# A hybrid decoder layer on one core: gates and scores in two row tiles of TensorE, another order of SyncE's loads, the last product by halves

## The chip, the cores and the metric

The kernel runs on one core of a Trainium2 chip. The metric is the device time of one execution in microseconds (us); lower is better. The engines are TensorE (PE, with PEld for its weight loads), VectorE (DVE), ScalarE (ACT), GpSimd (POOL) and SyncE (SP), which issues most DMAs. Each runs its own instruction stream in order; semaphores tie the streams together.

## The reference, cut to what matters

One layer on x of 2048 positions x 1024 channels, float32:

```python
h = rmsnorm(x, ln_gain);  z = h @ w_in                       # 1024 -> 4608 columns
q, k, v, g_attn, x_lru, g_lru = split(z)                     # 16 q heads, 4 kv heads, head_dim 64
q, k = partial_rope(q), partial_rope(k)
y_attn = swa_sink_attention(q, k, v, sinks) * silu(g_attn)   # window 128, blocks of 128
u = causal_depthwise_conv(x_lru, conv_w, conv_b)             # width 4
r = sigmoid(u @ w_r + b_r);  i = sigmoid(u @ w_i + b_i)      # 16 blocks of 64 x 64
a = exp(-8 * r * softplus(-lam))
h_t = a * h_(t-1) + sqrt(1 - a*a) * (i * u)                  # along the positions
y_lru = h * silu(g_lru)
out = rmsnorm(x + concat([rmsnorm(y_attn), rmsnorm(y_lru)]) @ w_out)
```

## The kernel before

**Precision.** Every product is made of float32 operands split in two parts, hi and lo, and takes three matmuls: hi x hi, hi x lo, lo x hi. The hi part is an ACT copy into the rounded type fp32r, the lo part a DVE (in places POOL) subtraction.

**Phase A** (`phase_a`) runs over 16 passes n: four quarters q of the sequence (512 positions) times four groups g (one kv head, four q heads, two 128-channel units u of the recurrent branch). A pass projects nine groups of 128 columns of w_in, each 24 matmuls of 128x512 (`project`, L1408): XL0, GL0, XL1 (inputs and gate of the recurrent branch), GA0, GA1 (attention gates), GL1, and KVG, Q0, Q1, which are already those of the next pass. In quarter 0 the weights come from w_in, are split on the chip (`split_w`) and both parts are stored to DRAM; from then on they are loaded back split. `split` and `split_next` tell the bodies which of the two it is. Results land in a ring of four PSUM banks, handed out by the list `R_XL0, R_GL0, ...`; `bank_free` waits until the user of the bank four places back has been drained.

TensorE's order in a pass is written out: XL0, GL0, XL1, score(0), gates(0), GA0, gates(1), score(1), GA1, turn_p(0), score(2), turn_x, GL1, weigh_v(0), turn_p(1), score(3), KVG, weigh_v(1), turn_p(2), Q0, weigh_v(2), turn_p(3), Q1, weigh_v(3), turn_v. turn_x transposes the next quarter's x; turn_p the probabilities of a block; weigh_v multiplies them by v.

- `score(b)` (L1437): per head two matmuls 128x128 by 128x256. `q_st` stacks the hi part of a head (64 rows) over its lo part, so that one matmul against k (k_hi stands twice, rows 0 to 63 and 64 to 127) yields two of the three products.
- `gates(u)` (L1469): two gates (r into bank R_R0/R_R1, i into R_I0/R_I1), three matmuls each. The weights of a gate are two blocks of 64x64 on the diagonal of a 128x128 tile whose other half is zero.
- ACT, `decays(u)`: tanh of r out of PSUM (L878), two activations of it (L884, L886), a square (L892), tanh of i (L895). Behind both decays: `s_copy(1)` (L826), `root_x` (L720, statistics of x, where q < 3), `lru_root` (L900).
- POOL, `lru_tail` (L618), then DVE, `lru_scan` (L1283), then `low_p(0)` (L1220), the lo part of the transposed probabilities, which weigh_v(0) needs.
- DVE, `softmax_a(b)`: a select (L1194) into s_sb and the row maximum (L1207); score(b+1) may overwrite ps_s only after the select of b. `norm_x` (L1016) normalises the next x, for turn_x.
- ACT `high_q` (L774) and DVE `low_q` (L1093) write q_st, two instructions each per q tile.
- SyncE: in each body XL0, GL0, x, XL1; in the body q = 3, g = 0 then the first loads of the output projection (y_scratch and three of w_out); then the gate weights gw_raw; in the last body of a quarter a wait for q_rot and the rope tables; then GA0, GA1, GL1 and the next pass's groups.

In the last body (n = 15) KVG, Q0 and Q1 have no work; the gaps hold chunks of the output projection instead, two a gap. A chunk is 6 matmuls of 128x512.

**Phase B** (`phase_b`): the output projection of 16 row blocks (8 steps m, two s), 96 matmuls each; DVE adds it to x with the scale of the norm (`add_group`, L1728), ACT squares (L1669), DVE normalises (L1738), POOL stores the block (L1657). Its weights lie where phase A's tiles were, so their loads start once phase A's stores have landed (`b.over`).

## Time and profile before

| | us |
|---|---|
| median of 3 runs | 1438.38 (1437.88 to 1440.07) |
| profiled execution | 1439.82 |
| its span, first to last instruction | 1438.2 |
| mean granted TensorE clock | 0.993 |
| PE busy | 1380.8 (96%) |
| PEld busy | 1136.5 (79%) |
| DVE busy | 1014.2 (71%) |
| ACT busy | 769.1 (53%) |
| POOL busy | 316.1 (22%) |

Busy time is time with at least one instruction of the engine under way; a matmul's record (0.39 us for 128x512) overlaps the next one's, so the pitch between starts is what a matmul costs in a stream. "[0.16 <-POOL ...]" behind a row means that the engine sat idle 0.16 us before it and that this instruction released it. Times count from the start of the span.

### The profile page before, as it was taken

The numbers are of one execution on the slowest core, as the hardware profiler recorded it, in microseconds if no ns is written. First come the engines' busy times: TensorE is split into PE (matmuls) and PEld (weight loads), VectorE is DVE, ScalarE is ACT, GpSimd is POOL, SyncE is SP. The second block draws the span as 40 slices with busy tenths as digits, with TensorE's granted clock in tenths as the row PEclk, the third lists the DMA queues.
The fourth block names the chain that finished last, engine by engine and source line by source line (L and its number), as shares of the span: only waits on it lengthen the run. The fifth ranks groups of instructions, "written<-read, shape, count | busy, mean of one in ns | idle before, by whom it ended". The sixth has DMA issues, their size and how long they took to land.

```text
span 1438.2 us, 21776 instructions
## 1 busy us (share of the span) xinstructions
PE 1380.8 (96%) x6464; PEld 1136.5 (79%) x6464; DVE 1014.2 (71%) x1729; ACT 769.1 (53%) x1552; POOL 316.1 (22%) x317
## 2 busy tenths in 40 slices
PE   5999999799999999999999999999989999999997
PEld 4778777688888888888888878788868888888886
DVE  4798989687877778787787868777886644344443
ACT  5677685747475664747566564747575322222221
POOL 2131423042322314232231414232230000000000
PEclk9999999999999999999999999999999999999999
DMA  8767674755546454554636374544717323233220
GB/s 221 243 240 246 237 248 162 253 202 193 182 155 197 157 198 165 176 185 154 222 120 235 126 244 151 194 160 167 231 53 257 119 86 117 73 102 101 74 87 29
DMA packets 151726, 243.24 MB, mean 169 GB/s; under 512 B 35440, under 2 KB 101232, under 8 KB 151664
## 3 DMA queue, kind: packets, MB, share of 16 engines
q1 hardware_dynamic: 144496, 217.33, 45.4%
q0 software_dynamic: 7168, 25.17, 5.2%
q8 instruction: 28, 0.46, 0.1%
q14 instruction: 34, 0.28, 0.1%
HBM read 179.55 MB, written 62.91 MB: 169 GB/s over the span
## 4 chain that ended last, share of the span: by engine, by line
PE 43%; DVE 21%; issue 18%; ACT 8%; POOL 3%; DMA 2%; SPq 2%; DVEq 1%; ACTq 1%; POOLq 0%
PE ring L1408 18%; PE acc_b L201 12%; PE ring L201 11%; DVE hs L1283 5%; POOL ri L618 2%; DVE p_lo L1220 2%; ACT p_sb L834 2%; DVE s_sb L1194 2%; DVE smax L1207 1%; PE ps_v L1458 1%; DVE cu L1249 1%; DVE o_sb L1229 1%; ACT cu L858 1%; DVE w_lo L1002 1%; ACT kc_ol L847 1%
## 5 line engine op out<-in xcount | busy, mean ns | idle before, releaser
L1408 PE MATMUL ring<-split,w_hi 128*128 128x512 f32 x2304 | 720.3, 394 | 8.1 <-DVE split L1022 7.5
L1408 PEld LDWEIGHTS ring<-split,w_hi 128*128 128x128 f32 x2304 | 427.9, 189 | 95.6 <-DVE split L1022 8.4
L1408 PE MATMUL ring<-split,w_lo 128*128 128x512 f32 x1152 | 450.8, 391 | 0.0
L1408 PEld LDWEIGHTS ring<-split,w_lo 128*128 128x128 f32 x1152 | 217.2, 189 | 46.7
L834 ACT ACTIVATE p_sb<-s_sb,smax 128x129 f32<-128x129 f32 x256 | 99.9, 392 | 124.6 <-DVE smax L1207 124.4
L618 POOL TENSOR_TENSOR ri<-ri,hs 128x512 f32<-128x512 f32 x32 | 54.8, 1732 | 395.6 <-ACT hs L900 395.6
L774 ACT ACTIVATE q_st<-qrot 64x512 fp32r<-64x512 f32 x64 | 40.4, 631 | 114.9 <-DVE qrot L1085 114.1
L1249 DVE SCALAR_TENSOR_TENSOR cu<-xl,prm,cu 128x512 f32<-128x512 f32 x96 | 72.2, 752 | 39.6 <-ACT cu L858 30.6
L1669 ACT ACTIVATE w_hi<-res 128x1024 fp32r<-128x1024 f32 x16 | 17.0, 1061 | 144.5 <-DVE res L1728 144.5
L201 PE MATMUL ring<-split,y_own 128*128 128x512 f32 x384 | 91.3, 392 | 0.0
L201 PE MATMUL acc_b<-wo_rest,y_own 128*128 128x512 f32 x384 | 89.8, 390 | 0.5 <-DVE wo_rest L162 0.5
L1283 DVE TENSOR_TENSOR_SCAN hs<-ra,h_carry,ri 128x512 f32<-128x512 f32 x32 | 73.7, 2302 | 17.0 <-POOL ri L618 15.2
L201 PEld LDWEIGHTS acc_b<-wo_rest,y_own 128*128 128x128 f32 x384 | 71.9, 188 | 15.8 <-DVE wo_rest L162 1.0
L1657 POOL DMA_DIRECT2D out_d<-res x16 | 8.6, 536 | 341.7 <-DVE res L1738 341.7
L201 PEld LDWEIGHTS ring<-split,y_own 128*128 128x128 f32 x384 | 71.4, 188 | 14.8
L1728 DVE SCALAR_TENSOR_TENSOR res<-acc_b,rms,res 128x1024 f32<-128x1024 f32 x16 | 20.5, 1284 | 88.2 <-PE acc_b L201 88.1
L628 POOL TENSOR_SCALAR_AFFINE_SELECT p_hi_c<-p_hi 128x512 fp32r<-128x512 f32 x64 | 55.3, 864 | 92.0 <-ACT p_hi L842 90.5
L639 POOL TENSOR_TENSOR rope<-rope 128x512 f32<-128x512 f32 x32 | 43.2, 1350 | 144.0 <-DVE rope L1080 144.0
L201 PE MATMUL ring<-split,w_hi 128*128 128x512 f32 x256 | 69.6, 394 | 0.0
L201 PE MATMUL acc_b<-wo_rest,w_hi 128*128 128x512 f32 x256 | 68.4, 389 | 0.0
L1235 DVE TENSOR_TENSOR ya<-ya,o_sb 128x256 f32<-128x256 f32 x64 | 66.0, 1031 | 2.2
L1437 PE MATMUL ps_s<-k_hi,q_st 128*128 128x256 f32 x256 | 66.5, 293 | 0.0
(195 smaller groups left out, 2486.0 us busy)
## 6 DMA issues: line engine op xcount, KB each, us to landing
w_hi<-w_split_scratch SPq DMA_DIRECT2D x108, 512.0 KB, 3.3
w_lo<-w_split_scratch SPq DMA_DIRECT2D x108, 512.0 KB, 4.3
w_split_scratch<-w_hi SPq DMA_DIRECT2D x36, 512.0 KB, 5.0
w_split_scratch<-w_lo SPq DMA_DIRECT2D x36, 512.0 KB, 5.7
w_raw<-w_in_d SPq DMA_DIRECT2D x32, 512.0 KB, 4.4
y_scratch<-hs POOLq DMA_DIRECT2D x32, 256.0 KB, 5.0
y_scratch<-ya POOLq DMA_DIRECT2D x16, 512.0 KB, 8.7
rows<-y_scratch SPq DMA_DIRECT2D x8, 1024.0 KB, 7.5
```

Source lines behind the costliest of these rows:

```text
L201: last = self.nc.tensor.matmul(banks[:, ACC[s, g][h], :], y[s][:, e, :], self.wo(e, low)[:, h * (D // 2):(h + 1) * (D // 2)], start=(e % ( ...
L618: nc.gpsimd.tensor_tensor(ri[u][:, :], ri[u][:, :], hs[u][:, :], ALU.mult).then_inc(*scan_in.one())
L628: nc.gpsimd.affine_select(out=dst[:, :, :], in_=f(src[:, :, :]), compare_op=ALU.is_ge, fill=0.0, base=0, pattern=[[0, GQ], [1, BLK]], chan ...
L639: nc.gpsimd.tensor_tensor(swp[:, :], swp[:, :], sinT[:, :], ALU.mult).then_inc(*q_sin.one())
L774: nc.scalar.activation(q_st[rows, 2 * j + half, :], qrot[rows, :], ACT.Copy).then_inc(*q_high.one())
L834: nc.scalar.activation(p_sb[:, b % 2, h, :], s_sb[:, b % 2, h, :], ACT.Exp, bias=smax[:, b % 2, 0, h:h + 1], accum_out=sden[:, b % 2, 0, h ...
L1194: nc.vector.copy_predicated(s, prev_mask[:, :, :], ps_s[:, :, 0:BLK]).then_inc(*s_sel.one())
L1235: nc.vector.tensor_tensor(y, y, o_sb[:, :, :], ALU.mult).then_inc(*ya_done.one())
L1249: stt(out=cu[u][:, :], in0=xl[:, tap:tap + T], scalar=prm[:, G, C_W0 + tap:C_W0 + tap + 1], in1=cu[u][:, :], op0=ALU.mult, op1=ALU.add).th ...
L1283: nc.vector.tensor_tensor_scan(hs[u][:, :], ra[u][:, :], ri[u][:, :], h_carry[:, G, :], ALU.mult, ALU.add).then_inc(*scanned.one())
L1408: last = mm(bank(r), w[:, i % WSLOTS, k, :], h[:, par, k, :], start=(k == 0 and j == 0), stop=(k == KC - 1 and j == 2))
L1437: last = mm(ps_s[:, h, :], q_st[:, h, b * BLK:(b + 1) * BLK], k[:, b * BLK:(b + 2) * BLK], start=st, stop=sp_)
```

## The change

Row tiles: `q_st` becomes `q_hi` and `q_lo`, each with two heads one above the other (rows 0 to 63 and 64 to 127). A matmul takes 64 rows; two that follow each other use different halves of the rows and write to different banks. The gate weights lose their zero halves: `gw_raw` is 128x128 per unit, lower rows [r | i], upper rows [i | r], so one bank holds r of channels 0 to 63 and i of the same channels, the other i and r of channels 64 to 127. ScalarE reads them by quarters of that pair. The heads stand in s_sb in the order 0, 2, 1, 3; sink_in and gather_o follow that. SyncE's order, norm_x's place in quarter 0, the chunks of the last body and the last row block of phase B change too. The diff, cut to its core:

```diff
-    def chunk(self, pe, banks, s, e):
+    def multiply(self, pe, banks, s, e, halves):
 g = e // (EC // 2)
 for j, (y, low) in enumerate(((self.y_hi, 0), (self.y_hi, 1), (self.y_lo, 0))):
-    for h in range(2):
+    for h in halves:
         last = self.nc.tensor.matmul(banks[:, ACC[s, g][h], :], y[s][:, e, :],
                                      self.wo(e, low)[:, h * (D // 2):(h + 1) * (D // 2)],
                                      start=(e % (EC // 2) == 0 and j == 0),
                                      stop=(e % (EC // 2) == EC // 2 - 1 and j == 2))
+return last
+
+    def chunk(self, pe, banks, s, e):
+last = self.multiply(pe, banks, s, e, range(2))
 if (e + 1) % (EC // 2) == 0:
...
 qrot = sb("qrot", [P, T])
-q_st = sb("q_st", [P, GQ, T], F32R)
+q_hi = sb("q_hi", [P, 2, T], F32R)
+q_lo = sb("q_lo", [P, 2, T], F32R)
...
         load(XL1, COL_XL + P)
+        sp.wait_ge(*gw_low.at(n, 0))
+        for j, w in enumerate((w_rgate, w_igate)):
+            for half in range(2):
+                rows = slice(half * BW, (half + 1) * BW)
+                at = (j + half) % 2
+                sp.dma_start(gw_raw[rows, :, at * BW:(at + 1) * BW],
+                             w[0, bass.ds(g * (2 * UNITS), 2 * UNITS), :, :].rearrange(
+                                 "(u h) c d -> c h u d", h=2)[:, half, :, :]
+                             ).then_inc(*gw_dma.one())
         if q == NQUART - 1 and g == 0:
...
-        sp.wait_ge(*gw_low.at(n, 0))
-        for j, w in enumerate((w_rgate, w_igate)):
-            for half in range(2):
-                rows = slice(half * BW, (half + 1) * BW)
-                sp.dma_start(gw_raw[rows, :, j, rows],
-                             w[0, bass.ds(g * (2 * UNITS), 2 * UNITS), :, :].rearrange(
-                                 "(u h) c d -> c h u d", h=2)[:, half, :, :]
-                             ).then_inc(*gw_dma.one())
+        load(GA0, COL_GA)
+        load(GA1, COL_GA + P)
+        load(GL1, COL_GL + P)
         if nxt_par != par and not last:
             sp.wait_ge(*q_rot.at(n, 0))
             load_tables((q + 1) * T)
-        load(GA0, COL_GA)
-        load(GA1, COL_GA + P)
-        load(GL1, COL_GL + P)
         if split_next:
...
         act.wait_ge(*scores.at(n, NBLK))
-        for half in range(2):
-            rows = slice(half * HD, (half + 1) * HD)
-            nc.scalar.activation(q_st[rows, 2 * j + half, :], qrot[rows, :], ACT.Copy
-                                 ).then_inc(*q_high.one())
+        nc.scalar.activation(q_hi[:, j, :], qrot[:, :], ACT.Copy).then_inc(*q_high.one())
...
             G = g * UNITS + u
-            act.wait_ge(*ring_ready.at(n, (R_R0, R_R1)[u] + 1))
+            lower, upper = slice(0, BW), slice(BW, P)
+            first, second = bank(R_R[u]), bank(R_I[u])
+
+            def take_i():
+                for to, ps in ((lower, first[upper, :]), (upper, second[lower, :])):
+                    nc.scalar.activation(ri[u][to, :], ps, ACT.Tanh, scale=0.5,
+                                         bias=prm[to, G, C_BI:C_BI + 1]).then_inc(*ring_act.one())
+
+            act.wait_ge(*ring_ready.at(n, R_I[u] + 1))
             act.wait_ge(*scanned.at(n, u + 1 - UNITS))
             act.sem_inc(settled, 1)
-            nc.scalar.activation(ra[u][:, :], bank((R_R0, R_R1)[u]), ACT.Tanh, scale=0.5,
-                                 bias=prm[:, G, C_BR:C_BR + 1]).then_inc(*ring_act.one())
-
-            act.wait_ge(*ring_act.at(n, FREED_BY_ACT.index((R_R0, R_R1)[u]) + 1))
+            for to, ps in ((lower, first[lower, :]), (upper, second[upper, :])):
+                nc.scalar.activation(ra[u][to, :], ps, ACT.Tanh, scale=0.5,
+                                     bias=prm[to, G, C_BR:C_BR + 1]).then_inc(*gate_r.one())
+
+            if u == 0:
+                take_i()
+            act.wait_ge(*gate_r.at(n, 2 * u + 2))
             act.wait_ge(*yl_out[u].at(n, 0))
...
             nc.scalar.activation(a2[:, :], ra[u][:, :], ACT.Square).then_inc(*decay.one())
-            act.wait_ge(*ring_ready.at(n, (R_I0, R_I1)[u] + 1))
-            act.sem_inc(settled, 1)
-            nc.scalar.activation(ri[u][:, :], bank((R_I0, R_I1)[u]), ACT.Tanh, scale=0.5,
-                                 bias=prm[:, G, C_BI:C_BI + 1]).then_inc(*ring_act.one())
+            if u == 1:
+                act.sem_inc(settled, 1)
+                take_i()
...
     def low_q(n, j):
-        for half in range(2):
-            rows = slice(half * HD, (half + 1) * HD)
-            other = slice((1 - half) * HD, (2 - half) * HD)
-            dve.wait_ge(*q_high.at(n, 2 * j + half + 1))
-            nc.vector.tensor_tensor(q_st[other, 2 * j + half, :], qrot[rows, :],
-                                    f(q_st[rows, 2 * j + half, :]), ALU.subtract
-                                    ).then_inc(*q_low.one())
+        dve.wait_ge(*q_high.at(n, j + 1))
+        nc.vector.tensor_tensor(q_lo[:, j, :], qrot[:, :], f(q_hi[:, j, :]), ALU.subtract
+                                ).then_inc(*q_low.one())
...
             dve.wait_ge(*ya_done.at(n, b))
-            pair = lambda ap, s: ap.rearrange("p (j s) t -> p s j t", s=2)[:, s]
+            pair = lambda ap, s: ap[:, 2 * s:2 * s + 2, :]
             for s in range(2):
...
             split_w(n, GL1)
+            norm_x(n, x_root.at(n, 1), x_rs, x_norm)
         softmax_a(1)
         if q < NQUART - 1:
-            norm_x(n, x_root.at(n, 1), x_rs, x_norm)
+            if not split:
+                norm_x(n, x_root.at(n, 1), x_rs, x_norm)
         elif g == 1:
...
             pe.wait_ge(*s_sel.at(n, b))
-            for h in range(GQ):
-                for k, st, sp_ in ((k_hi, True, False), (k_lo, False, True)):
-                    last = mm(ps_s[:, h, :], q_st[:, h, b * BLK:(b + 1) * BLK],
-                              k[:, b * BLK:(b + 2) * BLK], start=st, stop=sp_)
+
+            for j in range(2):
+                for i, (v, k) in enumerate(((q_hi, k_hi), (q_hi, k_lo), (q_lo, k_hi))):
+                    for half in range(2):
+                        rows = slice(half * HD, (half + 1) * HD)
+                        last = mm(ps_s[:, 2 * half + j, :], v[rows, j, b * BLK:(b + 1) * BLK],
+                                  k[rows, b * BLK:(b + 2) * BLK], start=(i == 0), stop=(i == 2))
             last.then_inc(*scores.one())
...
                 pe.wait_ge(*gw_low.at(n, 1))
-            for j in range(2):
-                r = ((R_R0, R_I0), (R_R1, R_I1))[u][j]
-                pe.wait_ge(*bank_free(n, r))
-                for i, (w, v) in enumerate(((gw_hi, u_hi), (gw_hi, u_lo), (gw_lo, u_hi))):
-                    last = mm(bank(r), w[:, u, j, :], v[:, :], start=(i == 0), stop=(i == 2))
-                last.then_inc(*ring_ready.one())
+
+            for half in range(2):
+                pe.wait_ge(*bank_free(n, (R_R, R_I)[half][u]))
+            for i, (w, v) in enumerate(((gw_hi, u_hi), (gw_hi, u_lo), (gw_lo, u_hi))):
+                for half in range(2):
+                    rows = slice(half * BW, (half + 1) * BW)
+                    ins = mm(bank((R_R, R_I)[half][u]), w[rows, u, :], v[rows, :], start=(i == 0), stop=(i == 2))
+                    if i == 2:
+                        ins.then_inc(*ring_ready.one())
...
             pe.wait_ge(*signals_b.y_low.at(0, 1))
-            for e in range(2):
+            for e in range(3):
                 pe.wait_ge(*signals_b.wo_low.at(e, 1))
...
         else:
-            for e in range(2, 4):
-                pe.wait_ge(*signals_b.wo_low.at(e, 1))
-                proj.chunk(pe, ring, 0, e)
+            pe.wait_ge(*signals_b.wo_low.at(3, 1))
+            proj.chunk(pe, ring, 0, 3)
+
+            pe.wait_ge(*ring_act.at(n, FREED_BY_ACT.index(R_I1) + 1))
+            pe.wait_ge(*ring_dve.at(n, FREED_BY_DVE.index(R_GL1) + 1))
+            pe.wait_ge(*signals_b.y_low.at(0, 2))
+            for e in range(2):
+                proj.chunk(pe, ring, 1, e)
         weigh_v(2)
         turn_p(3)
         if not last:
             project(n, Q1, nxt_par, split_next)
         else:
-
-            pe.wait_ge(*ring_act.at(n, FREED_BY_ACT.index(R_R1) + 1))
-            pe.wait_ge(*ring_dve.at(n, FREED_BY_DVE.index(R_GL1) + 1))
-            pe.wait_ge(*signals_b.y_low.at(0, 2))
-            for e in range(2):
+            for e in range(2, 4):
                 proj.chunk(pe, ring, 1, e)
...
-    sp.wait_ge(*b.y_low.at(STEPS, 0))
-    sp.wait_ge(*b.y_sq.at(STEPS, 0))
-    sp.sem_inc(b.y_in[0].sem, 16)
+
+    for h in range(2):
+        sp.wait_ge(b.half_normed, h + 1)
+        cols = slice(h * (D // 2), (h + 1) * (D // 2))
+        sp.dma_start(out[0, SEQ - P:, cols], res[:, 1, cols]).then_inc(b.half_out, 16)
+    sp.wait_ge(b.half_out, 32)
 @block.gpsimd
 def _(pool):
-    with pool.Fori(0, STEPS) as m:
+    def store(m, s):
+        pool.wait_ge(*b.normed.at(m, s + 1))
+        pool.sem_inc(b.settled, 1)
+        pool.dma_start(out[0, at_step(m, s), :], res[:, s, :]).then_inc(*b.stored[s].one())
+        pool.wait_ge(*b.stored[s].at(m, 1))
+        pool.sem_inc(b.res_free[s].sem, 1)
+
+    with pool.Fori(0, STEPS - 1) as m:
         for s in range(2):
-            pool.wait_ge(*b.normed.at(m, s + 1))
-            pool.sem_inc(b.settled, 1)
-            pool.dma_start(out[0, at_step(m, s), :], res[:, s, :]).then_inc(*b.stored[s].one())
-            pool.wait_ge(*b.stored[s].at(m, 1))
-            pool.sem_inc(b.res_free[s].sem, 1)
+            store(m, s)
+    store(STEPS - 1, 0)
...
     normalise(0, 1)
-    with dve.Fori(1, STEPS) as m:
+    def step(m, s):
+        mean_y(m, s)
+        proj.low_y(dve, m + s, 1 - s)
+        rms_y(m, s)
+        for g in range(2):
+            proj.sum_y(dve, m + s, 1 - s, g)
+        for g in range(2):
+            add_group(m, s, g)
+        normalise(m, s)
+
+    with dve.Fori(1, STEPS - 1) as m:
         for s in range(2):
-            mean_y(m, s)
-            proj.low_y(dve, m + s, 1 - s)
-            rms_y(m, s)
-            for g in range(2):
-                proj.sum_y(dve, m + s, 1 - s, g)
-            for g in range(2):
-                add_group(m, s, g)
-            normalise(m, s)
+            step(m, s)
+    m = STEPS - 1
+    step(m, 0)
+    mean_y(m, 1)
+    rms_y(m, 1)
+    add_group(m, 1, 0)
+    dve.wait_ge(*b.added.at(m, 3))
+    halves = [slice(h * (D // 2), (h + 1) * (D // 2)) for h in range(2)]
+    for h, cols in enumerate(halves):
+        dve.wait_ge(b.half_product, h + 1)
+        stt(out=res[:, 1, cols], in0=acc_of(1, 1)[:, h, :], scalar=rms[:, 1, 2, 1:2], in1=res[:, 1, cols],
+            op0=ALU.mult, op1=ALU.add).then_inc(b.half_added, 1)
+        dve.wait_ge(b.half_sq, h + 1)
+        if h == 0:
+            nc.vector.tensor_scalar(stat[:, 0, 1:2], stat[:, 0, 0:1], 1.0 / D, EPS, ALU.mult, ALU.add
+                                    ).then_inc(b.half_mean, 1)
+        else:
+            dve.wait_ge(b.half_mean, 1)
+            nc.vector.tensor_scalar(stat[:, 1, 1:2], stat[:, 1, 0:1], 1.0 / D, stat[:, 0, 1:2], ALU.mult, ALU.add
+                                    ).then_inc(b.half_mean, 1)
+    dve.wait_ge(b.half_root, 1)
+    nc.vector.reciprocal(stat[:, 1, 3:4], stat[:, 1, 2:3]).then_inc(b.half_root, 1)
+    dve.wait_ge(b.half_root, 2)
+    for cols in halves:
+        stt(out=res[:, 1, cols], in0=res[:, 1, cols], scalar=stat[:, 1, 3:4], in1=fgain[:, cols],
+            op0=ALU.mult, op1=ALU.mult).then_inc(b.half_normed, 1)
...
     begin(5)
-    for e in range(2, 4):
-        second(e)
-        begin(e + 4)
+    begin(6)
     second(4)
+    begin(7)
     second(5)
...
             begin(e + 4)
-    with pe.Fori(1, STEPS) as m:
+    def step(m, s, end=EC):
+        pe.wait_ge(*b.y_low.at(m, s + 1))
+        pe.wait_ge(*b.added.at(m, 2 * s + 2 - 4))
+        for e in range(end):
+            if e == 4:
+                sum_squares(m, s)
+            if e == EC // 2:
+                pe.wait_ge(*b.y_mean.at(m, 2 * s + 2))
+            proj.chunk(pe, banks(e), s, e)
+
+    with pe.Fori(1, STEPS - 1) as m:
         for s in range(2):
-            pe.wait_ge(*b.y_low.at(m, s + 1))
-            pe.wait_ge(*b.added.at(m, 2 * s + 2 - 4))
-            for e in range(EC):
-                if e == 4:
-                    sum_squares(m, s)
-                if e == EC // 2:
-                    pe.wait_ge(*b.y_mean.at(m, 2 * s + 2))
-                proj.chunk(pe, banks(e), s, e)
+            step(m, s)
+    step(STEPS - 1, 0)
+    step(STEPS - 1, 1, EC // 2)
+
+    pe.wait_ge(*b.y_mean.at(STEPS - 1, 4))
+    for h in range(2):
+        for e in range(EC // 2, EC):
+            last = proj.multiply(pe, acc, 1, e, (h,))
+        last.then_inc(b.half_product, 1)
```

## Rows read from the trace of the kernel before

**Rows 1.** Windows of four passes; span, then busy by engine, PEclk, DMA share, GB/s.

```profile
143.57:209.39 65.82, 63.92 (x306) 52.18 (x305) 60.50 (x98) 46.98 (x96) 19.24 (x18) 1.00 0.71 241
...
209.39:285.20 75.81, 66.99 (x316) 54.43 (x314) 62.61 (x102) 48.93 (x98) 21.57 (x20) 0.98 0.61 215
...
410.96:474.72 63.76, 63.40 (x306) 52.17 (x305) 49.50 (x89) 38.83 (x87) 18.32 (x19) 1.00 0.52 175
...
793.50:861.70 68.20, 64.89 (x305) 53.55 (x304) 49.10 (x86) 37.38 (x84) 18.24 (x18) 0.97 0.58 195
```

**Rows 2.** PE's timeline, one settled pass: start, duration, line, operation.

```profile
459.50 0.28 PE L1437 MATMUL ps_s<-k_hi,q_st 128*128 128x256 f32 x1
...
460.45 0.40 PE L1469 MATMUL ring<-u_hi,gw_hi 128*128 128x512 f32 x1
...
467.32 0.40 PE L1469 MATMUL ring<-u_hi,gw_hi 128*128 128x512 f32 x1
...
468.72 0.27 PE L1437 MATMUL ps_s<-k_hi,q_st 128*128 128x256 f32 x1
...
476.52 1.03 PE L1478 MATMUL ring<-ident,rows 128*128 128x128 f32 x8
...
484.08 0.50 PE L1458 MATMUL ps_v<-p_lo_c,dv_hl 128*128 128x512 f32 x1 [0.16 <-POOL p_lo_c L628]
...
505.42 0.47 PE L1458 MATMUL ps_v<-p_hi,v_hl 128*128 128x512 f32 x1 [0.20 <-DVE o_sb L1229]
```

**Rows 3.** ACT's timeline, the same pass.

```profile
461.55 0.69 ACT L878 ACTIVATE ra<-ring,prm 128x512 f32<-128x512 f32 x1
...
462.49 0.82 ACT L884 ACTIVATE hs<-ra,prm 128x512 f32<-128x512 f32 x1 [0.25 <-ACT ra L878]
...
468.42 0.69 ACT L878 ACTIVATE ra<-ring,prm 128x512 f32<-128x512 f32 x1 [0.30 <-PE ring L1469]
...
471.44 0.67 ACT L895 ACTIVATE ri<-ring,prm 128x512 f32<-128x512 f32 x1
...
472.01 0.59 ACT L826 ACTIVATE s_sb<-ps_s 128x512 f32<-128x512 f32 x1
```

**Rows 4.** POOL's and DVE's timelines, the same pass.

```profile
474.72 3.42 POOL L618 TENSOR_TENSOR ri<-ri,hs 128x512 f32<-128x512 f32 x2 [23.75 <-ACT hs L900]
...
477.02 2.19 DVE L1283 TENSOR_TENSOR_SCAN hs<-ra,h_carry,ri 128x512 f32<-128x512 f32 x1 [1.28 <-POOL ri L618]
...
482.05 0.68 DVE L1220 TENSOR_TENSOR p_lo<-ps_t,p_hi 128x512 fp32r<-128x512 f32 x1
```

**Rows 5.** Timelines of PE and ACT in quarter 0.

```profile
146.07 1.09 PE L1478 MATMUL ring<-ident,rows 128*128 128x128 f32 x8 [1.12 <-DVE rows L1016]
...
193.12 0.28 PE L1437 MATMUL ps_s<-k_hi,q_st 128*128 128x256 f32 x1
...
194.29 0.58 ACT L856 ACTIVATE xl<-ring 128x512 f32<-128x512 f32 x1
```

**Rows 6.** Groups by form, ACT and DVE: busy and mean ns, idle before.

```profile
L847 ACT ACTIVATE kc_ol<-ps_v 64x512 f32<-64x512 f32 x64 | 38.1, 595 | 6.9 <-PE ps_v L1458 5.4
...
L1093 DVE TENSOR_TENSOR q_st<-qrot,q_st 64x512 fp32r<-64x512 f32 x64 | 43.9, 686 | 19.4 <-ACT q_st L774 18.2
...
L1194 DVE COPY_PREDICATED s_sb<-prev_mask,ps_s 128x512 f32<-128x512 uint8 x64 | 47.1, 735 | 0.0
```

**Rows 7.** SyncE's waits (total, times, longest), ACT's timeline at two DMA waits.

```profile
SPq L530 <- DVE qrot L1085: 26.5, 3, 15.9
...
261.85 1.06 ACT L709 ACTIVATE w_hi<-w_raw 128x1024 fp32r<-128x1024 f32 x1 [7.49 <-DMA w_split_scratch<-w_lo]
...
844.02 0.63 ACT L906 ACTIVATE gw_hi<-gw_raw 128x512 fp32r<-128x512 f32 x1 [8.06 <-DMA gw_raw<-w_igate_d]
```

**Rows 8.** Timeline of the last row block.

```profile
1430.14 1.06 ACT L1669 ACTIVATE w_hi<-res 128x1024 fp32r<-128x1024 f32 x1 [10.33 <-DVE res L1728]
...
1433.97 0.53 POOL L1657 DMA_DIRECT2D out_d<-res  x1 [21.70 <-DVE res L1738]
```

More of the change, by code:

```diff
@@ L318, in phase_a @@
         h_carry = sb("h_carry", [P, LRU_W // P, 1])
-        gw_raw = sb("gw_raw", [P, UNITS, 2, P])
-        gw_hi = sb("gw_hi", [P, UNITS, 2, P], F32R)
-        gw_lo = sb("gw_lo", [P, UNITS, 2, P], F32R)
+        gw_raw = sb("gw_raw", [P, UNITS, P])
+        gw_hi = sb("gw_hi", [P, UNITS, P], F32R)
+        gw_lo = sb("gw_lo", [P, UNITS, P], F32R)
         ring = both.ring
@@ L372, in phase_a @@
         q_rot = signal("q_rot", 2, ahead=2)
-        q_high = signal("q_high", 4, ahead=4)
-        q_low = signal("q_low", 4, ahead=4)
+        q_high = signal("q_high", 2, ahead=2)
+        q_low = signal("q_low", 2, ahead=2)
         v_prev = signal("v_prev", 1, ahead=1)
@@ L611, in _ @@
             pool.sem_inc(primed, 1)
[L612 removed]
+            for ap in (k_carry, v_carry[:, :, :], x_carry[:, :, :], h_carry[:, :, :]):
                 nc.gpsimd.memset(ap, 0.0).then_inc(zeroed, 1)
@@ L905, in body @@
                 act.wait_ge(*ring_ready.at(n, R_I1 + 1 - NR))
-                nc.scalar.activation(gw_hi[:, :, :, :], gw_raw[:, :, :, :], ACT.Copy).then_inc(*gw_high.one())
+                nc.scalar.activation(gw_hi[:, :, :], gw_raw[:, :, :], ACT.Copy).then_inc(*gw_high.one())
                 if split:
@@ L1291, in body @@
                 dve.wait_ge(*gw_high.at(n, 1))
-                nc.vector.tensor_tensor(gw_lo[:, :, :, :], gw_raw[:, :, :, :], f(gw_hi[:, :, :, :]),
+                nc.vector.tensor_tensor(gw_lo[:, :, :], gw_raw[:, :, :], f(gw_hi[:, :, :]),
                                         ALU.subtract).then_inc(*gw_low.one())
@@ L1590, in signals_of_phase_b @@
     sem = lambda name: top.enter_context(nc.semaphore(name))
+    (b.half_product, b.half_added, b.half_sq, b.half_mean, b.half_root, b.half_normed, b.half_out) = (
+        sem("half_" + s) for s in ("product", "added", "sq", "mean", "root", "normed", "out"))
     b.over, b.fgain_in, b.settled = sem("phase_a_over"), sem("fgain_in"), sem("settled_b")
```

47 lines of the change are left out of this document (31 added, 16 removed).

## The prediction

> **What bounds the kernel now.** I read the page's busy shares first, then the windows of single passes, then the timelines of PE, ACT, POOL and DVE through one pass. A pass is one turn of the phase-A loop (16 of them, n = 0 to 15). TensorE looks like the bound: in a settled pass it is busy 63.40 of 63.76 us [rows 1]. That says little about what sets the pass. Follow it from the end of the third product, XL1 (459.50 is the next product's start): PE does score(0), gates(0), GA0, gates(1), score(1), GA1, turn_p(0), score(2), turn_x, GL1, and the last matmul of weigh_v(0) stands idle 0.16 us for GpSimd [rows 2]. In the same 24.6 us ScalarE works nearly without a pause: its only idle stretches are 0.25 us behind its own first tanh (461.55 to 462.49 is 0.94 us where 0.57 is its pace, 471.44 to 472.01) and 0.30 us for gates(1) [rows 3]. Then lru_root feeds GpSimd (ri, 474.72), GpSimd feeds the scan, which sat idle 1.28 us for it, the two scans run into p_lo (482.05), and p_lo into weigh_v(0) [rows 4]. So from XL1 to weigh_v(0) the path is ACT, POOL, DVE, with PE level beside it. From weigh_v(0) to weigh_v(3) DVE and ACT are level with PE as well: weigh_v(3) waits 0.20 us for o_sb [rows 2]. Only the rest (turn_v, XL0, GL0, XL1) is PE's alone. A pass is therefore two chains of equal length, and only what shortens both shortens it.
>
> The passes with split weights (n = 0 to 3) take 65.82 us, with DVE busy 60.50 [rows 1]; PE waits there 1.12 us for the normalised x at turn_x [rows 5]. Two passes are long: 75.81 and 68.20 us [rows 1].
>
> **Row tiles, on PE.** A score of one block is 8 matmuls at (460.45 - 459.50)/8 = 0.118 us; it becomes 6 pairs, each pair over two row tiles. If a pair costs what one matmul costs, it saves 2 x 0.118 = 0.24 us, 64 times: 15.1 us. Gates of one unit are 6 matmuls at (468.72 - 467.32)/6 = 0.233 us [rows 2]; 3 pairs save 0.70 us, 32 times: 22.4 us. No tiled matmul is in this trace, so a pair lies between one matmul and two; I take one, since the halves use different rows and banks. Each pass enters and leaves the tiled form four times (score(0) with gates(0), gates(1) with score(1), score(2), score(3)): 128 changes. The trace has none. From below: 0. From above: a matmul's record is 0.40 us at a pitch of 0.233, so waiting for the last one to end is 0.17 us, and a weight load that can't run ahead about as much again: 0.35 us. I take 0.15 us, nearest to the one drain. PE's own work falls by 37.5 - 19 = about 18 us.
>
> The Trainium skill ("TensorEngine Tiling (Array Packing)", Key Properties) says that changing the tiling mode drains the engine. No run here shows it yet; without a drain PE's work would fall by 37.5 us instead of 18. By the reading below, neither changes the forecast much; it weighs on the first rival.
>
> **What the tiles cost ScalarE.** Half of r and half of i now share a bank, so each tanh of 128 partitions becomes two of 64. The time of an ACT instruction follows the columns, not the partitions: 64x512 out of PSUM takes 595 ns [rows 6]. So decays(u) has two more instructions of 0.57 us pace, 4 a pass: 2.28 us. decays(0) hides 0.37 of it, because i's two halves fill the stretch in which it waits for its first tanh; the idle 0.30 us before gates(1)'s tanh hides the rest that can be hidden. s_copy(1), the square root and both lru_root come 2.28 - 0.67 = 1.6 us later [rows 3]. Nothing behind them has slack: GpSimd's ri, the scan and p_lo move by 1.6 us, and so does weigh_v(0) [rows 4]. On the way gates(1) isn't helped by PE being early: u_hi(1) comes 0.8 us later (four tanh of 0.57 each, 2.28 us, where 0.94 and i's own 0.57 stood), low_u behind it, so gates(1) starts about 0.1 us later than 467.32, not 0.6 earlier. The PE time saved in score(0), gates(0), gates(1), score(1) and score(2) becomes PE idle time. In the second part score(3) is 0.24 - 2 x 0.15, about nothing, and the chain through DVE stays.
>
> What gets shorter elsewhere is off that path: high_q is two ACT instructions fewer, low_q two DVE instructions of 686 ns fewer [rows 6], both between weigh_v(3) and XL1's end, where PE alone decides; gw_hi and gw_lo are half as wide, with ACT waiting for conv(0) right behind.
>
> Passes n = 4 to 11: 8 x 1.6 = +12.8 us (bounds: 0 if the path had slack, 2.3 each if nothing is hidden). n = 12 to 15: no norm there, a little more idle on ACT; 1.4 each, +5.6.
>
> Passes n = 0 to 3: here ACT has no idle stretch before gates(1)'s tanh, so the square root comes 2.28 - 0.37 = 1.9 us later. norm_x now goes ahead of softmax_a(1). It no longer waits behind select and maximum (0.74 and about as much), but score(2) needs that select, so behind norm_x come select (0.74), score(2) (0.71) and entering the tiles (0.15), all ahead of turn_x [rows 6]. That puts turn_x 1.9 + 0.2 = 2.1 us later, and its present wait of 1.12 us [rows 5] is not cured. Some 0.8 us comes back: ACT takes XL1 at 194.29, 1.17 us after PE started on score(0); I allow 0.3 for the way from PE to ACT. The rest is DVE being late, and the two low_q relieve it (1.4 us). Net 1.3 each, +5.2 (bounds 0 and 2.5).
>
> **SyncE's order.** In body n = 3 load_tables waits for q_rot (SyncE waits 15.9 us at worst there) with the load of GA0's weights and XL0's store behind it; ACT's split of GA0 then sat 7.49 us [rows 7]. PE's idle time in that window is 75.81 - 66.99 = 8.8 us against 1.9 in its neighbour, and its mean clock 0.98 makes 1.5 more [rows 1]: 8.4 us lost. Afterwards GA0, GA1, GL1 go out first, and the tables still have some 30 us until turn_k. I count -8.4. At n = 12 y_scratch and three w_out loads are issued ahead of gw_raw; ACT sat 8.06 us for it [rows 7]. Idle 3.3 against 0.4 us and clock 0.97 make 2.9 + 2.0: -4.9. Both moved groups pass only loads of SyncE's own queue; x's load stays ahead. Each could give nothing if the queue were slow for another reason.
>
> **Last body and end.** Three chunks in a gap fill waits for p_lo and o_sb, but the wo_rest loads, which start only when phase A's stores are done, decide some 20 us later, and weigh_v(3), which sets these stores, isn't earlier: -0.5 (bounds 0 and -2.7, two chunks). At the end the last add, square (1.06 us) and normalisation are done by halves, the first half of add and square during the product; about 0.6 + 0.5 go, the store is no longer a GpSimd one, issued 3.84 us after the square began [rows 8], and its second half is half as large: -1.8 (bounds -0.8 and -3). Priming one more signal: 0.1.
>
> **Sum.** +12.8 + 5.6 + 5.2 - 8.4 - 4.9 - 0.5 - 1.8 = +8.0 us on the profiled execution's 1439.8 (span 1438.2): 1447.8. That execution is 1.4 us above the median of 1438.4, so 1446.
>
> **Rivals.** *PE is the bound after all* (27%): the ACT chain has room that I don't see, and the 18.5 us of PE work show, with 13.3 and 2.3 beside: 1438 - 34 = 1404, from 1385 without a cost of changing to 1420 with 0.27 each. For it: PE busy 99.4% of a pass. Against it: the idle 0.16, 0.20 and 1.28 us [rows 2, 4], which name POOL and DVE as what was late. *A pair's two weight loads don't overlap* (13%): the transposes, with 128 columns both loaded and streamed, go at (1.03 - 0.28)/7 = 0.11 us [rows 2], so a load may itself take that, and a score pair would take 0.22 us. Scores then take 1.3 us instead of 0.95; score(0) is on the path to ACT's first tanh (+0.6), score(3) adds 0.5: 16 x 1.1 = +17, 1463. It decides from the point where a pair costs over 0.16 us, and gates, at 0.23, would still gain.
>
> This is also what the skill's "TensorE: Matmul & The Clock Gate", section LDWEIGHTS, amounts to: a load takes 128 columns at 1.2 GHz, an estimate of 107 ns, however few rows it has. The transposes' pitch agrees; that two loads of different row tiles queue is not shown here.
>
> *The tiles don't run together at all* (5%): 12 x 0.118 and 6 x 0.233 us again; +2.2 a pass over the forecast, 1481.
>
> **Chances.** The forecast's case has 55%, 1440 to 1455 by itself. No change means within 0.2% (2.9 us), about what can be measured here. The forecast puts a fifth of its weight there or below; half of PE's gain showing would land just below 1438. Faster 30%, same 15%, slower 55%. Range 1418 to 1463: it takes in the upper half of the first rival's neighbourhood and the second, and leaves out a PE-bound 1404 and the serial tiles.
>
> **What the profile would show.** If right: each decays has four 64x512 tanh of about 0.6 to 0.7 us; settled passes last 65.2 to 65.4 us; PE's busy time falls by 15 to 25 us, and new waits of 0.5 to 1.5 us stand at gates(1) (for u_lo), turn_x (for rows) and weigh_v(0) (for p_lo). The 7.49 and 8.06 us waits are gone. If PE is the bound: passes of about 62.5 us and no such waits. If loads queue: tiled scores of one block span over 1.2 us. It would be wrong altogether if the halves of tanh came in under 0.4 us each, or if a settled pass were under 63.7 us.

## The result and the profile after

The changed kernel takes 1462.99 us (median of 4 runs) against 1439.22 for the kernel before: a ratio of 1.0167 (95% interval 1.015 to 1.0185). It is slower, by 23.8 us. Its profiled execution took 1462.87 us, span 1461.3, 23.1 us longer than before.

Windows of four of its passes, each from GpSimd's first lru_tail to the next pass's (span, then busy by engine, granted clock, DMA share, GB/s); they answer [rows 1]:

```profile
146.69:214.90 68.21, 63.39 (x320) 51.69 (x320) 58.46 (x98) 48.34 (x98) 19.06 (x18) 0.97 0.68 233
...
214.90:282.89 67.99, 63.46 (x320) 51.68 (x320) 58.43 (x98) 48.39 (x98) 19.06 (x18) 0.97 0.64 227
...
416.68:482.93 66.25, 62.70 (x320) 50.07 (x320) 48.13 (x88) 39.94 (x89) 18.31 (x19) 1.00 0.48 169
...
813.55:879.94 66.39, 62.63 (x321) 50.36 (x322) 47.52 (x85) 38.73 (x86) 18.23 (x19) 1.00 0.54 200
```

The settled pass is 66.25 us where it was 63.76, 2.49 longer. A quarter-0 pass went from 65.82 to 68.21. Between the same two events the long pass of n = 3, 73.47 us before (its window in [rows 1] ends a little later), is 67.99, and that of n = 12 went from 68.24 to 66.39.

TensorE in one settled pass (start, duration, line, operation, idle before it), against [rows 2]; L1459 is the score, L1493 the gates, "x2" a pair of tiles:

```profile
464.99 0.39 PE L1427 MATMUL ring<-split,w_lo 128*128 128x512 f32 x1
...
465.31 0.38 PE L1459 MATMUL ps_s<-k_hi,q_hi 64*128 64x256 f32 x2
...
466.00 0.28 PE L1459 MATMUL ps_s<-k_hi,q_lo 64*128 64x256 f32 x2
...
466.12 0.40 PE L1493 MATMUL ring<-u_hi,gw_hi 64*128 64x512 f32 x2
...
466.59 0.40 PE L1493 MATMUL ring<-u_hi,gw_lo 64*128 64x512 f32 x2
...
466.91 0.73 PE L1427 MATMUL ring<-split,w_hi 128*128 128x512 f32 x2
...
467.48 0.39 PE L1427 MATMUL ring<-split,w_lo 128*128 128x512 f32 x1
...
473.86 0.50 PE L1493 MATMUL ring<-u_hi,gw_hi 64*128 64x512 f32 x2 [1.22 <-DVE u_lo L1274]
...
474.65 0.28 PE L1459 MATMUL ps_s<-k_hi,q_hi 64*128 64x256 f32 x2
...
484.04 1.09 PE L1503 MATMUL ring<-ident,rows 128*128 128x128 f32 x8 [1.32 <-DVE rows L1034]
```

A score is six pairs at (466.00 - 465.31)/5 = 0.138 us, of which the first takes 0.22 and the others 0.117; a gates call is three pairs at 0.233. So a pair costs what one matmul did. Entering takes 464.99 to 465.31, 0.32 us where 0.23 is the pitch, and 0.10 more in the first pair. Leaving takes 466.59 to 466.91, 0.32 again, and the first two full matmuls take 0.57 (466.91 to 467.48) where two take 0.46 in the rest of the product. A round trip is about 0.4 us, a change 0.2.

The Trainium skill ("TensorEngine Tiling (Array Packing)", Key Properties) says that changing the mode drains the engine; the trace agrees, with 0.2 us a change.

The same pass on ScalarE, against [rows 3]; L895 and L888 are the halves of r's and i's tanh, two to a row:

```profile
467.26 1.40 ACT L895 ACTIVATE ra<-ring,prm 64x512 f32<-64x512 f32 x2
...
468.68 1.40 ACT L888 ACTIVATE ri<-ring,prm 64x512 f32<-64x512 f32 x2
...
470.11 0.82 ACT L903 ACTIVATE hs<-ra,prm 128x512 f32<-128x512 f32 x1
...
475.07 1.40 ACT L895 ACTIVATE ra<-ring,prm 64x512 f32<-64x512 f32 x2
...
478.80 1.38 ACT L888 ACTIVATE ri<-ring,prm 64x512 f32<-64x512 f32 x2
...
480.20 0.60 ACT L834 ACTIVATE s_sb<-ps_s 128x512 f32<-128x512 f32 x1
```

Two halves last 1.40 us and the next instruction starts 1.40 to 1.43 after their start: each half occupies ScalarE for 0.70, where a whole tanh has a pace of 0.57. From the take of XL1 (465.55) to the square root (482.12) it is 16.57 us; before it was 14.08.

GpSimd and VectorE, against [rows 4]:

```profile
482.93 2.11 POOL L629 TENSOR_TENSOR ri<-ri,hs 128x512 f32<-128x512 f32 x1 [26.96 <-ACT hs L918]
...
485.17 2.21 DVE L1300 TENSOR_TENSOR_SCAN hs<-ra,h_carry,ri 128x512 f32<-128x512 f32 x1 [1.26 <-POOL ri L629]
```

Behind ScalarE the chain is as long as before: the scan starts 2.24 us after ri, where it was 2.30.

What TensorE waited for in the whole execution (total us, times, longest), and its busy time on the page:

```profile
PE ring L1493 <- DVE u_lo L1274: 17.6, 16, 1.9
...
PE ps_v L1480 <- DVE p_lo L1237: 15.0, 13, 3.4
...
PE ps_s L1459 <- DVE s_sb L1211: 14.5, 4, 3.7
...
PE ring L1503 <- DVE rows L1034: 10.4, 8, 1.3
```

```profile
PE 1369.9 (94%) x6720; PEld 1108.0 (76%) x6720; DVE 984.8 (67%) x1709; ACT 785.0 (54%) x1583; POOL 313.7 (21%) x315
```

Its work fell, from 1380.8 to 1369.9 us, and it stands idle longer: for gates(1), for the normalised x, for p_lo, and in quarter 0 for the select ahead of score(2). The clock falls behind these last four waits, of 3.6 us each. Behind each of them the granted clock stands at 0.50, the lower of its two levels (1.2 of 2.4 GHz), for some 3.4 us, and over these passes it is 0.97, as the first two windows above show. In the kernel before, where TensorE waits 1.12 us in such a pass [rows 5], it is 1.00 [rows 1].

The end, on VectorE and ScalarE, against [rows 8] (the first half of add and square lies beside the product):

```profile
1449.77 0.75 DVE L1836 SCALAR_TENSOR_TENSOR res<-acc_b,rms,res 128x512 f32<-128x512 f32 x1 [4.12 <-PE acc_b L203]
...
1455.14 0.75 DVE L1836 SCALAR_TENSOR_TENSOR res<-acc_b,rms,res 128x512 f32<-128x512 f32 x1 [3.67 <-PE acc_b L203]
...
1455.92 0.63 ACT L1747 ACTIVATE w_hi<-res 128x512 fp32r<-128x512 f32 x1 [4.64 <-DVE res L1836]
```

From the last square to the end of the span it is 5.4 us, where it was 8.1.

### The profile page after: what moved, and what is told of

Read it like the earlier page. It is cut to its first block, busy times and chain, and to the rows that moved or that the text cites. A ratio compares the mean times of both kernels' runs of the same rounds, so it can differ in the third digit from the quotient of the medians.

```text
span 1461.3 us, 22249 instructions
## 1 busy us (share of the span) xinstructions
PE 1369.9 (94%) x6720; PEld 1108.0 (76%) x6720; DVE 984.8 (67%) x1709; ACT 785.0 (54%) x1583; POOL 313.7 (21%) x315
## 4 chain that ended last, share of the span: by engine, by line
PE 60%; issue 14%; DVE 11%; ACT 11%; POOL 2%; DMA 1%; ACTq 1%; DVEq 0%; POOLq 0%
PE ring L1427 32%; PE acc_b L203 12%; PE ring L203 11%; DVE hs L1300 4%; PE ps_v L1480 3%; POOL ri L629 2%; ACT p_sb L842 2%; ACT ra L895 1%; DVE p_lo L1237 1%; ACT ri L888 1%; ACT ra L905 1%; DVE s_sb L1211 1%; DVE o_sb L1246 1%; PE ps_s L1459 1%; ACT hs L903 1%
## 5 line engine op out<-in xcount | busy, mean ns | idle before, releaser
L783 ACT ACTIVATE q_hi<-qrot 128x512 fp32r<-128x512 f32 x32 | 20.3, 634 | 115.0 <-DVE qrot L1103 115.0
L1252 DVE TENSOR_TENSOR ya<-ya,o_sb 128x256 f32<-128x256 f32 x64 | 66.1, 1033 | 2.2
L1246 DVE TENSOR_TENSOR o_sb<-ps_v,kc_ol 64x256 f32<-64x256 f32 x128 | 53.5, 418 | 6.7 <-ACT kc_ol L855 3.1
```

What stands on the lines that cost most here:

```text
L783: nc.scalar.activation(q_hi[:, j, :], qrot[:, :], ACT.Copy).then_inc(*q_high.one())
L1246: nc.vector.tensor_tensor(o_sb[s * HD:(s + 1) * HD, :, :], pair(ps_v[0:HD], s), pair(o_low, s), ALU.add).then_inc(*o_sum.one())
L1252: nc.vector.tensor_tensor(y, y, o_sb[:, :, :], ALU.mult).then_inc(*ya_done.one())
```

## The experiments

**ScalarE or TensorE?** Four kernels. First, the changed kernel with gates whole, as before; scores stay tiled.

```diff
-for half in range(2):
-    ins = mm(bank((R_R, R_I)[half][u]), w[rows, u, :], v[rows, :], ...)
+for j in range(2):
+    last = mm(bank(r), w[:, u, j, :], v[:, :], ...)
```

> The changed kernel with the gates as before (two 128-row products per unit, tanh over 128 partitions); scores stay in row tiles, and SyncE's order, norm_x's place, the last body and the last row block stay changed. Theory ACT (ScalarE's eight 64-partition tanh a pass, at a pace of 0.71 us instead of 0.57, lengthen the path XL1 to weigh_v(0)): settled passes fall from 66.25 back to 63.6 to 63.9 us, the total to 1425 (1420 to 1431). Theory TILES (entering and leaving the tiled form, or PE's own work, lengthens the pass): three of four changes of form a pass remain, settled passes stay above 65.3, total above 1448.

Measured: 1422.46 us, ratio 0.9887 (0.987 to 0.9903). The tiled gates cost 40 us, and the rest of the change is a gain.

Second, the kernel before with the cost to ScalarE alone: each tanh of decays in two halves of 64 partitions, no tiles.

```diff
-nc.scalar.activation(ra[u][:, :], bank(r), ACT.Tanh, ...)
+for p in (slice(0, 64), slice(64, 128)):
+    nc.scalar.activation(ra[u][p, :], bank(r)[p, :], ACT.Tanh, ...)
```

> The kernel before, each of the four tanh of decays split into partitions 0 to 63 and 64 to 127, nothing else; no row tiles. Theory ACT: settled passes 66.2 to 66.8 us instead of 63.76, total 1476 to 1488. Theory TILES: nothing of the cost comes from ACT, settled passes below 64.3, total below 1446.

Measured: 1486.14 us, ratio 1.0336 (1.0318 to 1.0353); a settled pass is 66.57 us. The halves alone make the kernel 47 us slower.

Third, the changed kernel with one 128-partition tanh per bank. Half of r and half of i share a bank, so it takes them mixed.

> The changed kernel with one tanh of 128 partitions per bank in place of two halves each; it then mixes r and i and leaves that part of the computation wrong, all work of PE being that of the changed kernel. Theory ACT: settled passes 63.2 to 63.8 us, no lower, because the chain ACT, POOL, DVE is then as long as before and PE's saved 2 us a pass turn into waits; total 1420 to 1428. Theory TILES: stays within 3 us of 1463. Rival PE (with ACT out of the way PE's saving shows): settled passes below 62.5, total below 1408.

Measured: 1416.68 us, ratio 0.9852 (0.9835 to 0.9868), settled pass 63.38 us. The time is 3 us below the ACT theory's range, on the side of its rival but 9 us short of it. TensorE's busy time:

```profile
PE 1363.7 (96%) x6720; PEld 1100.9 (78%) x6720; DVE 981.7 (69%) x1709; ACT 736.2 (52%) x1519; POOL 313.6 (22%) x315
```

That is 17.1 us less than before: the forecast's "about 18". Against the first experiment (1422.5) it is worth 5.8 us in all, so most of TensorE's saving is hidden even where nothing is added on ScalarE.

Fourth, the kernel before with each of these tanh in two halves by columns, 128x256 each.

> The kernel before, each of the four tanh of decays split into columns 0 to 255 and 256 to 511 over all 128 partitions: as many instructions as in the split by partitions. If what costs is that 64 partitions take the time of 128 and don't overlap with the next instruction: pace about 0.35 us each, settled passes 64.0 to 64.6, total 1443 to 1452. If it is the number of instructions and their semaphores: as the split by partitions, settled passes above 65.8, total above 1470.

Measured: 1443.35 us, ratio 1.0039 (1.0025 to 1.0053). Four more ACT instructions a pass cost 4 us when the tanh are split by columns and 47 when they are split by partitions: it is not the number of instructions.

**What makes a half cost 0.70.** Three kernels built on the one with one tanh per bank (1416.7), each with four ACT instructions a pass more, into a spare tile `dup`.

```diff
+nc.scalar.activation(dup[p1, :], bank(r)[p1, :], ACT.Tanh, ...)
-nc.scalar.activation(ra[u][:, :], bank(r), ACT.Tanh, ...)
+nc.scalar.activation(ra[u][p2, :], bank(r)[p2, :], ACT.Tanh, ...)
```

p1 and p2 are both all partitions:

> As the kernel with one 128-partition tanh per bank (1416.7, r and i mixed), with each of these four tanh a pass done twice, whole, the first time into a spare tile: eight 128x512 tanh instead of the changed kernel's eight 64x512. Theory: whole tanh follow each other at 0.57 us; the four added ones cost 2.28 less the 0.3 to 0.5 us that was idle, a settled pass of 65.2 to 65.4 us and 1443 to 1449 in all, so eight whole ones are cheaper than eight halves (1463). Rival: the pace of 0.70 comes from reading one bank twice in a row or from the number of tanh, not from the halves: then the same 66.2 us and 1460 to 1465.

both partitions 0 to 63:

> As the kernel with one tanh per bank, but each tanh on partitions 0 to 63 only and done twice, the first time into a spare tile; the upper half of r and i is left out. Eight 64x512 tanh a pass, all on the same partitions. Theory: an instruction on 64 partitions does not overlap the next one, whichever partitions that has: two last 1.38 to 1.40 us, a settled pass 66.0 to 66.4 us, 1458 to 1466 in all. Rival: it is the change from partitions 0 to 63 to partitions 64 to 127 that stops the overlap: two last 1.26 us and the time is that of the doubled whole tanh, 1443 to 1449.

p1 partitions 0 to 63, p2 all:

> As the kernel with one tanh per bank, with a 64x512 tanh on partitions 0 to 63 into a spare tile ahead of each whole one. Theory: it is the half one whose end the next instruction awaits: each added one costs 0.70 us, so a settled pass is 65.7 to 65.9 us and the total 1451 to 1456. Rival: only two halves in a row fail to overlap; then a half costs what a whole one does, 65.2 to 65.4 us and 1443 to 1449.

Measured: 1450.8, 1452.3 and 1449.3 us, ratios 1.0078, 1.0082 and 1.007 (intervals within 0.002), and in all three the same settled pass, 65.40 to 65.42 us at a clock of 1.00. Eight whole tanh cost less than the changed kernel's eight halves, as the first theory had it. The theories of the second and third fell; their rivals stand. The settled pass and the rows below decide that: the totals lie 2, 3 and 0.3 us above the ranges of 1443 to 1449, and the traces show a granted clock of 0.95 to 0.97 in most passes of quarter 0, in the second also in that of n = 12 (0.95, 70.39 us), which no expectation allowed for. The second's four runs spread from 1448 to 1461 us, and its trace is of the longest. ScalarE in the second (64x512, all on partitions 0 to 63):

```profile
467.16 0.69 ACT L888 ACTIVATE dup<-ring,prm 64x512 f32<-64x512 f32 x1
...
467.75 0.67 ACT L890 ACTIVATE ra<-ring,prm 64x512 f32<-64x512 f32 x1
...
468.32 0.68 ACT L895 ACTIVATE dup<-ring,prm 64x512 f32<-64x512 f32 x1
...
468.89 0.68 ACT L897 ACTIVATE ri<-ring,prm 64x512 f32<-64x512 f32 x1
...
469.46 0.81 ACT L905 ACTIVATE hs<-ra,prm 128x512 f32<-128x512 f32 x1
```

They start 0.57 to 0.59 us apart, also where the bank changes (from r's to i's, 467.75 to 468.32). A half is no dearer than a whole tanh when the next instruction begins at the same partition.

So it is the change of the first partition, from 0 to 64 or back, that keeps the next instruction out until the last has ended. Is it the partitions written or those read? Two more, on the changed kernel: unit 0's four halves ordered by the partitions written; then both units'. In outline:

```diff
-ra[0:64], ra[64:128], ri[0:64], ri[64:128]     # tanh in this order
+ra[0:64], ri[0:64], ra[64:128], ri[64:128]     # read: 0, 64, 64, 0, as before
```

> The changed kernel with the four tanh of unit 0 in another order: r and i into partitions 0 to 63 first, then r and i into 64 to 127 (two changes of the partitions written instead of four; the partitions read go 0, 64, 64, 0 instead of 0, 64, 64, 0 by the order r, r, i, i). Theory: a change of the partitions written costs 0.13 us, so the four take 2.54 instead of 2.80 us, the settled pass 65.98 instead of 66.25 and the whole 1459 (1457 to 1461). Rival: a change of the partitions read costs it too; then the pace stays 0.70 where read or written partitions change, which they do at each of the four, and nothing moves: 1463.

Measured: 1464.45 us, ratio 1.0173 (1.0156 to 1.019): no gain. ScalarE there:

```profile
467.89 0.68 ACT L895 ACTIVATE ra<-ring,prm 64x512 f32<-64x512 f32 x1
...
468.60 0.69 ACT L898 ACTIVATE ri<-ring,prm 64x512 f32<-64x512 f32 x1
...
469.31 0.68 ACT L895 ACTIVATE ra<-ring,prm 64x512 f32<-64x512 f32 x1
...
470.02 0.68 ACT L898 ACTIVATE ri<-ring,prm 64x512 f32<-64x512 f32 x1
...
470.72 0.81 ACT L903 ACTIVATE hs<-ra,prm 128x512 f32<-128x512 f32 x1
```

All pitches are 0.70 to 0.71. From the first to the second only the partitions read from PSUM change (0 to 64), so that is enough. From the second to the third these stay at 64 and the partitions written change, and with them those of the bias operand, `prm[to, ...]`, and the bank, which by the rows above costs nothing. Whether the output or the bias does it was not told apart.

> As the one before, in both units; unit 1's two tanh of i stand beside those of r, which also fills the 0.23 us in which ScalarE waits for its own tanh of r. Theory: 0.27 + 0.27 + 0.23 = 0.77 us a pass off the chain, 66.25 - 0.77 = 65.5, and 1463 - 12 = 1451 (1448 to 1455). Rival (partitions read count as well): only the 0.23 goes, 1459 to 1460. Rival 2: i ahead of unit 1's decays makes GpSimd and VectorE later than it makes ScalarE earlier: 1463 or more.

Measured: 1473.99 us, ratio 1.0252 (1.0228 to 1.0276). Rival 2 holds in its sign: unit 1's decays come behind i, and TensorE now waits 24.7 us for the select ahead of a score, 16 times, in quarter 0 up to 4.9 us (3.7 in the changed kernel); these passes take 69.3 to 70.6 us. The settled pass is no longer where the clock holds: 66.1 us at 1.00, 0.2 less than in the changed kernel, near the 0.23 of the first rival. But in five of the seven passes from n = 4 on the granted clock is 0.97, and they take 66.8 to 67.3 us. In one of them it falls behind TensorE's 2.09 us wait at turn_x (1.32 in the changed kernel); in another the same wait left it at 1.00, so what decides between the two stays open.

**SyncE's order.** The kernel before with that alone, in outline:

```diff
 load(XL1, COL_XL + P)
+gw_raw's four loads
 ... first loads of the output projection
-gw_raw's four loads; load_tables; load GA0, GA1, GL1
+load GA0, GA1, GL1; load_tables
```

> The kernel before with SyncE's order alone changed (the gate weights' loads ahead of the output projection's, GA0, GA1 and GL1 ahead of the rope tables); everything else as before. Theory: the two long passes shrink by what the traces of both kernels show, 7.2 to 8.4 us at n = 3 and 4.1 to 4.9 at n = 12: 1439 - 12.3 = 1427 (1425 to 1429), other passes unchanged at 63.75 and 65.82 us. Rival: in the changed kernel the long passes shrank because their neighbours had grown and the loads had more time; then less than half is left here, 1433 or more.

Measured: 1427.64 us, ratio 0.9908 (0.9893 to 0.9923), or -13.2 us. Its windows of n = 3 and n = 12, with the clock back at 1.00:

```profile
208.75:273.80 65.05, 63.35 (x304) 52.00 (x303) 60.42 (x98) 46.94 (x96) 19.24 (x19) 1.00 0.67 237
...
784.43:848.66 64.23, 63.34 (x305) 52.30 (x304) 49.12 (x86) 37.61 (x84) 18.26 (x18) 1.00 0.57 207
```

They were 73.47 and 68.24 us: -8.4 and -4.0. Some of the 4.0 is the clock's, and that part varies: in the trace of the last kernel below (the end alone), whose code is the old one there, the pass of n = 12 took 66.32 us at a clock of 1.00, against 68.24 at 0.97.

**norm_x first.** The changed kernel with norm_x behind softmax_a(1) again:

> The changed kernel with norm_x back behind softmax_a(1) in quarter 0; everything else as changed. Theory (the prediction's step): the move costs 0.2 us a pass, four times, and the wait only stands at another place: 1462 (1459 to 1465), with TensorE's 3.6 us waits at score(2) replaced by longer ones at turn_x. Rival 1: the 14.5 us that TensorE waits at score(2) in quarter 0 are the price of the move: 1449 to 1455. Rival 2: the move helps, because turn_x waits for it: 1466 or more.

Measured: 1464.22 us, ratio 1.0164 (1.015 to 1.0178): the same. The wait for x (L1501) and that for the select (L1457) swap; they were 10.4 and 14.5:

```profile
PE ring L1501 <- DVE rows L1034: 17.2, 12, 1.7
...
PE ps_s L1457 <- DVE s_sb L1211: 7.2, 4, 1.9
```

The same on the kernel with whole gates:

> As the kernel with whole gates and tiled scores (1422.5), but norm_x back behind softmax_a(1) in quarter 0. Theory: TensorE's waits at score(2) (2.9 us in all) go, and waits at turn_x of the size of the kernel before (4.5 us in all) come: 1424 (1422 to 1426). Rival, from the prediction's 0.2 us a pass: 1421.7. Rival 2: in the kernel before, quarter 0's passes took 65.82 us and here they take 65.0; if the move gave all of that, 1422.5 + 3.2 = 1425.7.

Measured: 1424.32 us, ratio 0.9888 (0.9872 to 0.9903), that is 0.9887 again. The move is worth nothing.

**Tiled scores alone.** Scores whole as well; SyncE's order, the move, last body and end stay.

> The changed kernel with scores and gates both as before: what is left of the change is SyncE's order, norm_x first, three chunks a gap and the end by halves. Theory: tiled scores save nothing, because entering and leaving the tiles costs what the pairs save (with tiled scores and whole gates a block takes 1.43 us from turn_p's start to turn_x against 1.39 before, and a settled pass 63.87 us against 63.75): 1421 (1419 to 1424), and the settled pass is 63.75 again. Rival, the prediction's terms: 2 x 0.118 us saved per block less 0.15 for each change of form; that is worth up to 6 us of TensorE's time in 64 blocks, which would show now that TensorE is nearly the bound: 1426 to 1430.

Measured: 1425.02 us, ratio 0.9895 (0.988 to 0.991), against 0.9887 with tiled scores: no difference that can be told. A settled pass is 63.77 us against 63.87 with tiled scores, as the theory had it; the total lies between the two expected ranges. In quarter 0 tiled scores help, 65.01 us a pass against 65.66, and VectorE's work there is 1.6 us less. One block between turn_p(0) and turn_x, with tiled scores, then in the kernel before (whose turn_x starts at 476.52 [rows 2]):

```profile
463.26 0.60 PE L1454 MATMUL ps_t<-ident,p_sb 128*128 128x128 f32 x4
...
463.79 0.39 PE L1446 MATMUL ps_s<-k_hi,q_hi 64*128 64x256 f32 x2
...
464.69 1.09 PE L1487 MATMUL ring<-ident,rows 128*128 128x128 f32 x8
```

```profile
475.13 0.60 PE L1445 MATMUL ps_t<-ident,p_sb 128*128 128x128 f32 x4
...
475.49 0.36 PE L1437 MATMUL ps_s<-k_hi,q_st 128*128 128x256 f32 x1
```

1.43 us against 1.39. TensorE's busy time, with tiled scores and then without:

```profile
PE 1382.5 (97%) x6720; PEld 1121.5 (79%) x6720; DVE 985.8 (69%) x1709; ACT 742.0 (52%) x1519; POOL 314.0 (22%) x316
```

```profile
PE 1378.4 (97%) x6464; PEld 1134.8 (80%) x6464; DVE 1008.6 (71%) x1725; ACT 765.9 (54%) x1551; POOL 314.7 (22%) x316
```

Where a score stands by itself, the round trip takes back the 0.24 us that the pairs save.

**The end.** Last body and end alone on the kernel before:

> The kernel before with the last body (three chunks a gap) and the end by halves alone. Theory (the prediction's terms): -0.5 and -1.8 us, a ratio of 0.9984, 1437. Rival: the two kernels' traces, in which the stretch from the last body's lru_tail to the end is 2.5 to 3.4 us shorter: 0.9977. Rival 2: the end's second small DVE and ACT steps eat what the halves save: 1.000.

Measured: 1437.17 us, ratio 0.9984 (0.9975 to 0.9993): the sum of the forecast's two terms.

**The best of both** is the change without its tiled gates, 1422.46 us, ratio 0.9887. Without any tiles (0.9895), or with norm_x back (0.9888), it is the same within the intervals.

## Why the prediction had the sign and missed the size

The direction and the bound were right: slower, because ScalarE's chain sets the first part of a pass and TensorE's savings turn into idle time. The size was not, +8 us forecast and +23.1 in the profiled execution, and one term did most of it. A second, the clock in quarter 0, was not in the sum at all.

**The failed step** is "two more instructions of 0.57 us pace, 4 a pass: 2.28 us", drawn from "the time of an ACT instruction follows the columns, not the partitions". The duration does follow the columns: 0.68 us on 64 or on 128 partitions. But 0.57 is a duration less an overlap with the next instruction, and the overlap is lost where that one reads from or writes to another first partition. Eight halves at 0.70 are 5.6 us, not 4.6: 1.0 more a pass. The settled pass then comes to 1.6 + 1.0 = +2.6 (2.49 measured). Over n = 4 to 11 that is +19.1 where +12.8 was forecast (with 2.25 put down for the pass of n = 12, whose loads also changed), over n = 12 to 15 +7.4 where +5.6 was, 0.8 of it in a pass at a clock of 0.97. A bound stood in the rows: the durations, 0.67 and 0.69 each [rows 3], without any overlap.

**Quarter 0.** It is +11.1 where +5.2 was forecast. 1.3 and the same 1.0 make 2.3 a pass; the first two passes measured 2.40 and 2.39. That the figures meet so closely is in part luck, because the forecast had no term for TensorE's clock, which falls behind the 3.6 us waits. In the kernel with unit 0's halves reordered, the first of these passes kept a clock of 1.00 in spite of the same wait and took 67.74 us, against 68.23 at 0.97 in the changed kernel, and its second took 69.24 at 0.95. So about 0.5 us of the 2.4 is the clock's, by this estimate from two traces, and without it the pass would be 1.9 longer. The rest lies ahead of the first lru_tail (0.7) and in the pass after the long one (3.2 instead of 2.4, at 0.97 as well). The halves alone cost 3.47 a pass here (69.29 us in the kernel before with halves, at 0.98), 1.1 more than the whole change, so what the forecast let come back (0.8) did come back. "Norm_x ahead costs 0.2" was right within what can be told: undoing it changes nothing.

**The upper bound per pass**, "2.3 each if nothing is hidden", rested on the same pace, so the range had no room above 1463, and the result fell on its edge.

**Right in size:** the pair at the cost of one matmul; the change of form (0.15 taken, 0.2 measured, inside 0 to 0.35); TensorE's work (18 forecast, 17.1 where ScalarE's halves are away and the clock holds); SyncE's order, -8.4 and -4.9 forecast, 12.4 in the windows and 13.2 in the runs measured alone (in the changed kernel -12.0, against passes that are longer there). The -8.4 at n = 3 has some luck in it: it was worked out from a window that ends 2.3 us behind the pass, 75.81 us instead of 73.47. Last body and end: -2.3 against a ratio of 0.9984 and 2.5 us in the trace. Added up: 11.1 + 19.1 + 7.4 - 12.0 - 2.5 = +23.1.

**The rivals.** *PE is the bound* is false for the change, but half true of the kernel: with the halves away the whole gain is 22 us, of which SyncE's order and the end are 15, and the tiles' 17 us of TensorE work bring some 7. *Loads that don't overlap* and *tiles that don't run together* are false: 0.117 and 0.233 us a pair. Of the marks named in advance, the duration of a half, the new waits (1.22 us at gates(1), 1.32 at turn_x) and the end of the 7.49 and 8.06 us waits are there. The settled pass of 65.2 to 65.4 us is not, nor is the fall of TensorE's busy time by 15 to 25 us: it fell by 10.9. Matmuls at half clock stay busy longer; with one tanh per bank, where quarter 0 keeps a clock of 1.00, it is 6.2 us lower still.
